# Down weights queued ahead of gate and up in the expert blocks, one down half in three passes

## The reference

```
probs = softmax(ht @ w_router)                     # 512 tokens, 16 experts
e_idx = top 2 inside the best of 4 groups
...
def expert_block(args):
    xb, e = args                                   # rows of one block, its expert
    return (silu(xb @ w1[e]) * (xb @ w3[e])) @ w2[e]
# w1, w3: 1024 x 512 (gate, up); w2: 512 x 1024 (down)
...
out = segment_sum(ys * slot_w, slot_tok)
```

## Time and profile before

| | |
|---|---|
| runs of the kernel before | 3133.07 us median of 3 (3132.41 to 3136.28) |
| the profiled execution | 3134.4 us, its span 3132.8 us |
| PE busy | 2995.8 us (96%) |
| DVE busy | 1664.4 us (53%) |
| ACT busy | 1266.9 us (40%) |
| POOL busy | 1091.5 us (35%) |
| moved | 501.22 MB, mean 160 GB/s |
| expert blocks | from about 2637 us of the span to 3093 us |

### The profile page before, as it was taken

How to read it: one execution, slowest core, us unless ns; L and a number is a source line. 1 busy time by engine, 2 the same in 40 slices (tenths; PEclk the granted TensorE clock), 3 DMA queues, 4 the chain that set the end, 5 groups by cost and what they waited for, 6 DMA issues and landing times. The chain is left out here.

```text
span 3132.8 us, 35850 instructions
## 1 busy us (share of the span) xinstructions
PE 2995.8 (96%) x13604; PEld 2278.2 (73%) x13604; DVE 1664.4 (53%) x2818; ACT 1266.9 (40%) x1920; POOL 1091.5 (35%) x538
## 2 busy tenths in 40 slices
PE   6899999999989999999999999999999998999998
PEld 4676677888866667788887677878777886666664
DVE  5577673222246758432213663656777146666664
ACT  4365434223245553422324454323444234554443
POOL 1242344444423324344342654444444431000001
PEclk9999999999999999999998999999999999999999
DMA  6122563433421137474332333733432325899995
GB/s 231 54 61 75 181 199 111 148 127 101 118 81 55 61 101 242 127 305 149 95 115 77 132 122 115 225 90 113 120 112 68 94 101 229 329 381 382 381 381 208
DMA packets 188504, 501.22 MB, mean 160 GB/s; under 512 B 20080, under 2 KB 98032, under 8 KB 172224
## 3 DMA queue, kind: packets, MB, share of 16 engines
q1 hardware_dynamic: 165808, 417.24, 39.4%
q0 software_dynamic: 13200, 49.32, 4.0%
q10 hardware_dynamic: 9344, 32.61, 3.0%
HBM read 463.83 MB, written 35.29 MB: 159 GB/s over the span
## 5 line engine op out<-in xcount | busy, mean ns | idle before, releaser
L3089 POOL TENSOR_TENSOR w_lo<-ring,w_hi 128x1024 fp32r<-128x1024 f32 (+1 forms) x375 | 900.2, 2403 | 1370.3 <-ACT w_hi L1574 1370.1
L745 PE MATMUL banks<-h_lo,w_hi 128*128 128x512 f32 x2104 | 824.8, 392 | 0.0
L1574 ACT ACTIVATE w_hi<-ring 128x1024 fp32r<-128x1024 f32 (+1 forms) x375 | 388.7, 1038 | 545.9 <-DMA ring<-in_w_all 471.0
L744 PE MATMUL banks<-hx_hi,w_hi 128*128 128x512 f32 (+2 forms) x1400 | 588.4, 420 | 12.6 <-DVE tmp L2532 6.9
L746 PE MATMUL banks<-hx_hi,w_lo 128*128 128x512 f32 (+2 forms) x1400 | 551.2, 394 | 0.0
L745 PEld LDWEIGHTS banks<-h_lo,w_hi 128*128 128x128 f32 x2104 | 397.2, 189 | 86.7 <-issue 10.2
L744 PEld LDWEIGHTS banks<-hx_hi,w_hi 128*128 128x128 f32 (+2 forms) x1400 | 264.7, 189 | 126.9 <-issue 56.5
L746 PEld LDWEIGHTS banks<-hx_hi,w_lo 128*128 128x128 f32 (+2 forms) x1400 | 264.3, 189 | 60.4 <-issue 0.2
L744 PE MATMUL banks<-hf_hi,w_hi 128*128 128x512 f32 x704 | 274.7, 390 | 0.7 <-DVE h_lo L2255 0.7
L746 PE MATMUL banks<-hf_hi,w_lo 128*128 128x512 f32 x704 | 274.0, 389 | 0.0
L2574 DVE TENSOR_TENSOR arena<-sgs,banks 128x512 f32<-128x512 f32 x44 | 30.3, 689 | 314.5 <-PE banks L746 314.5
(11 more groups left out here) (462 smaller groups left out, 5163.1 us busy)
## 6 DMA issues: line engine op xcount, KB each, us to landing
ring<-in_w_all SPq DMA_DIRECT2D x352, 512.0 KB, 3.9
arena<-in_w_all SPq DMA_DIRECT2D x26, 2048.0 KB, 14.0
arena<-in_w_all SPq DMA_DIRECT2D x100, 512.0 KB, 4.9
ring<-in_w_all SPq DMA_DIRECT2D x46, 1024.0 KB, 7.4
arena<-in_w_all SPq DMA_DIRECT2D x25, 1024.0 KB, 9.3
x<-in_w_all SPq DMA_DIRECT2D x23, 1024.0 KB, 9.5
abuf<-in_w_all SPq DMA_DIRECT2D x32, 512.0 KB, 5.0
routed<-abuf POOLq DMA_DIRECT2D x1, 12288.0 KB, 52.2
```

Of the source, the lines that this page charges most:

```text
L744: pe.matmul(bank[0:m, :], upper, hi, start=first, stop=False)
L745: pe.matmul(bank[0:m, :], upper, lo, start=False, stop=False)
L1574: act.activation(hi_at(u)[:, 0:n], raw_at(u)[:, 0:n], ACT.Copy).then_inc(w_upper, 1)
L3089: pool.tensor_tensor(lo_at(u)[:, 0:n], raw_at(u)[:, 0:n], hi_at(u)[:, 0:n], ALU.subtract)\
```

## The change

- SP: inside the loop over blocks, `down_in(b-1)` now stands ahead of `gate_and_up(b)`.
- PE: in blocks 1 to 21 the first down half (columns 0 to 511) stays a float32 product, the second (512 to 1023) is taken in three passes of halves, 12 matmuls; it waits for `hid_split`. Blocks 0 and 22 keep `down_block`.
- ACT: `upper_down(b-1)` makes the upper halves of the hidden rows (512 columns) and of the second down half (two of 1024). It stands at the start of `step(b)`, ahead of `gate_half(b)`, and waits for `hidb` and for the down load.
- DVE: `lower_down(b-1)` makes the lower halves (one of 512, two of 1024) at the start of `block_step(b)`, ahead of unit 0's, and waits for all three ACT instructions. The lower half of the weights is written over the weights; the upper halves have room of their own in `arena`.

```diff
@@ SP
             for b in range(3, N_BLK):
+                down_in(b - 1, (b - 1) % 2, b - 1)
                 if b == E_N:
                     router_told(sp, "experts_known")
                 gate_and_up(b)
-                down_in(b - 1, (b - 1) % 2, b - 1)
             down_in(N_BLK - 1, 0, N_BLK - 1)
@@ PE
+            def down_half(half, par):
+                for k in range(4):
+                    mm = pe.matmul(sc_b[half], hidb[:, k * P:(k + 1) * P],
+                                   down[par][:, k * D + half * SEQ:k * D + (half + 1) * SEQ],
+                                   start=(k == 0), stop=(k == 3))
+                return mm
+            def split_down_block(b, par):
+                pe.wait_ge(sem("wd_in%d" % par), 8 * (b - par) + 16)
+                pe.wait_ge(sem("hidden_in"), b + 1)
+                pe.wait_ge(sem("yd2_done"), b + 1)
+                down_half(0, par)
+                pe.wait_ge(sem("hid_split"), 3 * b + LAYERS * FF_T)
+                for k in range(4):
+                    rows_hi, rows_lo = hidb_hi[:, k * P:(k + 1) * P], hidb_lo[:, k * P:(k + 1) * P]
+                    pe.matmul(sc_b[1], rows_hi, down_hi[:, k, :], start=(k == 0), stop=False)
+                    pe.matmul(sc_b[1], rows_hi, down_lo[par][:, k, :], start=False, stop=False)
+                    mm = pe.matmul(sc_b[1], rows_lo, down_hi[:, k, :], start=False, stop=(k == 3))
                 mm.then_inc(sem("d_done"), 1)
@@ ACT
+            def upper_down(b, par):
+                act.wait_ge(sem("hidden_in"), b + 1)
+                act.activation(hidb_hi, hidb, ACT.Copy).then_inc(sem("hid_upper"), 1)
+                act.wait_ge(sem("wd_in%d" % par), 8 * (b - par) + 16)
+                for k in range(0, 4, 2):
+                    act.activation(down_hi[:, k:k + 2, :], down_raw[par][:, k:k + 2, :], ACT.Copy).then_inc(sem("hid_upper"), 1)
-            def step(b):
+            def step(b, par=None):
                 act.wait_ge(sem("hidden"), b)
+                if par is not None:
+                    upper_down(b - 1, par)
                 gate_half(b)
@@ DVE
+            def lower_down(b, par):
+                dve.wait_ge(sem("hid_upper"), 3 * b + LAYERS * FF_T)
+                TT(hidb_lo, hidb, hidb_hi, SUB).then_inc(sem("hid_split"), 1)
+                for k in range(0, 4, 2):
+                    TT(down_lo[par][:, k:k + 2, :], down_raw[par][:, k:k + 2, :], down_hi[:, k:k + 2, :], SUB)\
+                        .then_inc(sem("hid_split"), 1)
-            def block_step(b, par, first=False):
+            def block_step(b, par, first=False, split=True):
+                if split:
+                    lower_down(b - 1, 1 - par)
                 lower_weights(b + 1, (0,))
```

More of the change, by code:

```diff
@@ L468, in two_blocks @@
         htok = part(QT, D)
+        wdown_at = cursor[0]
         wdown = part(4 * D)
@@ L480, in two_blocks @@
         down = [wdown, flat(merged2)]
+        blocks_of = lambda v: v.rearrange("p (a b) -> p a b", b=D)[:, :, SEQ:D]
+        down_raw = [blocks_of(v) for v in down]
+        down_lo = [blocks_of(halves("down_lo%d" % n, "arena", at, 4 * D)) for n, at in enumerate((wdown_at, 0))]
+        split_at = -(-cursor[0] // 64) * 64
+        down_hi = halves("down_hi", "arena", split_at, 4, SEQ)
+        hidb_hi, hidb_lo = (halves("hidb_%s" % n, "arena", split_at + at, SEQ) for n, at in (("hi", 4 * SEQ), ("lo", 5 * SEQ)))
+        print("SPLIT", split_at, ARENA, shared_end)
         SLOT = 4 * UNIT
@@ L1486, in down_block @@
                 pe.wait_ge(sem("yd2_done"), b + 1)
[L1487 to L1491, removed]
+                down_half(0, par)
+                down_half(1, par).then_inc(sem("d_done"), 1)
+            def split_down_block(b, par):
+                pe.wait_ge(sem("wd_in%d" % par), 8 * (b - par) + 16)
+                pe.wait_ge(sem("hidden_in"), b + 1)
+                pe.wait_ge(sem("yd2_done"), b + 1)
+                down_half(0, par)
+                pe.wait_ge(sem("hid_split"), 3 * b + LAYERS * FF_T)
[4 more added lines that the diff above has]
+                    mm = pe.matmul(sc_b[1], rows_lo, down_hi[:, k, :], start=False, stop=(k == 3))
                 mm.then_inc(sem("d_done"), 1)
@@ L1506, in _ @@
                 if b == 2:
-                    down_block(1, 1)
+                    split_down_block(1, 1)
                 turn_hidden(b)
@@ L1514, in _ @@
                     rows_in(b + 1, n)
-                    down_block(b - 1, n)
+                    split_down_block(b - 1, n)
                     turn_hidden(b)
@@ L2179, in step @@
                 upper_weights(b + 1, (2, 3))
-            for b in (1, 2):
-                step(b)
+            step(1)
+            step(2, 1)
             with act.Fori(1, (N_BLK - 1) // 2 - 1) as i:
                 for n in range(2):
-                    step(2 * i + (n + 1))
-            step(N_BLK - 2)
+                    step(2 * i + (n + 1), n)
+            step(N_BLK - 2, 0)
             act.wait_ge(sem("hidden"), N_BLK - 1)
+            upper_down(N_BLK - 2, 1)
             gate_half(N_BLK - 1)
@@ L3051, in _ @@
             for b in (1, 2):
-                block_step(b, b % 2, True)
+                block_step(b, b % 2, True, b == 2)
             with dve.Fori(1, (N_BLK - 1) // 2 - 1) as i:
@@ L3056, in _ @@
             block_step(N_BLK - 2, 1)
+            lower_down(N_BLK - 2, 1)
             gated_block(N_BLK - 1)
```

## The result

The changed kernel takes **3147.1 us** (median of 7 runs, 3141.3 to 3152.1) against 3134.3 us before (7 runs, 3131.5 to 3139.3): a ratio of 1.0041, with a 95% interval from 1.0031 to 1.0051. It is slower by 0.4%, 12.8 us. I had forecast 3125.4 us, a gain, with a range up to 3136.0. The prediction is wrong in sign.

What follows compares the result with a forecast made beforehand. It took PE and the DMA engines as both full; blocks of 18.85 us instead of 19.18 over 19 periods save 6.3 us, plus 1.4 from blocks 1 and 21: -7.7 us, giving 3125.4 us, range 3118.0 to 3136.0.

Steps and rivals of the forecast that it cites:

- the second path: From unit 1's landing to the next block's lowered rows, 4.65 us; gives a 19.0 us block, or 17.5 in another.
- Part 3: Work put on DVE: 2.9 us a block plus standstill for ACT's 2.5; serial paths give 18.8 to 19.0 us a block.
- Part 4: SP's queue: down load issued ahead of unit 0, in time for ACT, but queue depth lost: a quarter microsecond idle a block.
- Part 1: Second down half on PE as 12 matmuls: saves 0.70 us a block, 14.7 us at most over 21 blocks.
- The gap: DMA idleness between unit 3 and the later down load: 0.25 us a block, ends nothing and 0.8 us.
- What the DMA engines can do: Time the transfers need for a block's 7.37 MB: between 17.3 and 19.1 us, taken as 18.6.
- full already: Rival: transfers need 19.1 us a block, so the loop stays there; 3130.2 us in all, chance 0.30.
- The long serial path: From ACT's start on unit 3 through hidden rows, ACT and DVE work to the next block's lowered rows: some 17.2 us.
- DVE as full as PE: With the new lowering work and the standstill for ACT, DVE comes to 18.3 us a block.
- The wait of PE on the lowered rows: Sign of being right: PE waits some 0.4 us a block for the lowered rows.
- The gap case: Rival: transfers need 19.1 us and also idle 0.5 before the down load; 19.6 a block, 3139.7 us, chance 0.14.
- The first rival: PE remains the bound in the block loop, so all 14.7 us are gained: 3118.4 us, chance 0.18.

Runs made afterwards that it cites:

- e1: Kernel before the change with only the new SP order (down load ahead of gate and up), no split and no new ACT or DVE work: 3141.6 us.
- e2: Changed kernel with SP's old order, the down load behind unit 3: 3134.1 us, ratio 0.9994 to the kernel before.
- e6: Changed kernel with SP's old order and the next block's rows raised and lowered ahead of unit 1: 3120.9 us, ratio 0.9948 to the kernel before.
- e7: Changed kernel with rows ahead of unit 1 and the second down half multiplied as float32, new ACT and DVE work kept: 3131.5 us.
- e9: Changed kernel with the down load issued between units 1 and 2: 3166.9 us, ratio 1.0101 to the kernel before.
- e5: Kernel before the change with only the rows raised and lowered ahead of unit 1: 3129.7 us, ratio 0.9982.
- e4: Changed kernel, new order kept, with the next block's rows raised and lowered ahead of unit 1: 3120.4 us, ratio 0.9949 to the kernel before.
- e3: Changed kernel with all new ACT and DVE work and waits, but PE multiplies the second down half as float32: 3141.3 us, ratio 1.0010.

## Why the prediction was wrong

**The step that failed: the second path.** I found the loop through unit 1 in Part 3 (unit 1 lands, the rows are lowered 4.65 us later) and closed it with "The change does not shorten this path". That was true, and the wrong question: the change lengthened it. I took unit 1's landing at S + 12.8 to 14.3 as given, though Part 4 moved 2 MB directly ahead of units 0 and 1 and Part 1 asked for the same bytes in less time. On average it lands at S + 15.4 in after, S + 13.9 in before. L went from 8.1 to 9.15 us, which by 10.6 + L raises the waiting period from 18.7 to 19.75. Five blocks at half clock, whose unit 1 is issued 1.3 to 1.7 us later, add 0.43 us to the mean, and the four that end otherwise 0.14: that makes the 20.32. It took the order and the split together: either alone leaves L at 7.9 or 8.1 (e1, e2). What in the queue makes L grow when both are there was not isolated.

**The gap (Part 4) was put in the wrong sum.** I priced the lost depth of the queue at 0.25 us of DMA idleness a block, added to what the transfers need. The idleness is real (98 GB/s at 2814, DMA share 0.94 against 0.99), but it isn't an addend: it delays exactly the unit on which the start of the next block hangs, which delays the issue of the unit after that. My upper end for it, 0.8 us a block, was under the 1.5 us by which 20.33 exceeds 18.85.

**What the DMA engines can do** was mis-sized too: I took 18.6 us a block from the distance of two landings and gave 0.30 to "full already" on a share of 0.99. e6 moves the same 7.37 MB in 18.45 us at 398 GB/s. At a share of 0.99 the engines had more to give; they went at the pace at which they were asked. By the Trainium skill, "DMA: Bandwidth & Descriptors", section Specifications, some 358 GB/s is a core's limit from HBM, a stack's 716 divided by its two cores; e6's row of a kernel on one core disagrees, as the earlier trace rows did. Its fabric ceiling of 435 GB/s is contradicted by no row of 320 us here.

**What held.** The passes (Part 1): 0.70 us a block foreseen, 19.10 to 18.45 = 0.65 measured from e7 to e6, and 11 us of the at most 14.7 in the median. The long serial path: 17.2 us foreseen, 17.2 read in e9, and it ends ten of e2's blocks, at a period near the 19.0 that I gave it. DVE as full as PE at 18.3 us: in e6 DVE copies the hidden rows at 2783.30 and again at 2801.59, 18.29 us apart, and starves nobody. PE doesn't wait for hid_split in after. The work on ACT and DVE is covered where the rows hang on unit 0 (e7 against e5). The wait of PE on the lowered rows was foreseen at 0.4 us a block and is 22.3 / 18 = 1.2, and that did not hold.

**The rivals.** The gap case had the right sign and the right place, SP's queue between unit 3 and the down load. Its price was 19.6 us a block where 20.3 came, its mechanism (the engines' capacity plus a pause) was not the one found, and its condition, that the transfers need over 18.7 us, was not met: they need at most 18.45. Its chance of 0.14 was too low, because I had tied the danger to capacity and not to latency. The first rival, PE stays the bound, is what e4 and e6 became: 3120.4 and 3120.9 us against its 3118.4. It needed one edit that the change doesn't have.

**The clock** was in no part of the sum. In after the five waits of 2.0 us and more at the start of a block went with the five drops and the shorter ones with none, so those waits were dearer than their own length. The length of one wait doesn't decide it: e3 has PE idle for 2.2 us and e9 for 2.9 (2803.2 to 2806.1), each at a clock of 1.00 and with no drop behind it.

```profile
2784.50:2786.70 2.20, 0.07 (x1) 0.00 (x0) 2.20 (x4) 1.88 (x3) 0.00 (x0) 1.00 0.86 227
```

**Two slips** in the prediction changed no step. By its own sum, 18.75 to 19.0 us a block is 3123.5 to 3128.2 us and not 3122.5 to 3127.3; and slice 35 of the page has 8 tenths and 329 GB/s, so that 381 holds from slice 36 on the earlier trace rows.

**What stays open.** The 5 to 6 us that the order alone costs (e1) show in the median and in the scatter but not in its one profile. The granted clock doesn't explain them: e1's executions of 3139.4, 3141.2 and 3141.7 us have the 0.983 of its fastest. Its profile has one block behind unit 1, 19.67 us with L at 9.12; more of these, as in e3, would do it, but no profile shows them. How the 12.4 us of added PE busy time (343.65 against 18 x 18.40 = 331.2) divide beyond the 8.2 us of half clock was not tried. The gain of e6 over e2 wasn't divided between the two paths that the edit relieves. A down load cut in two transfers with a unit between them was not tried either.

## What to carry to other kernels

Before you move a transfer in a queue, write down for each transfer behind it who waits for its landing and whether that wait closes a loop with its own issue; such a loop costs latency, and a faster engine doesn't shorten it. When a faster engine brings nothing, look for what its next stage really hangs on: here, taking the rows out from behind a 1 MB unit they had no need of was worth 0.2% alone and turned the loss of 0.4% into a gain of 0.5%. A DMA share of 0.99 says that the engines had work, not that they could do no more.

## What the runs showed of the hardware that I had not expected

- The same transfers, the same packets: 381 GB/s at a share of 0.99 before, 398 GB/s at 1.00 in e6, over 320 us or more each. The share doesn't measure how near the rate is to its limit.
- PE's clock fell to 1.2 GHz for 3.4 us some time *after* PE had resumed in four of the five drops: 1.4 us (idle until 2794.6, half clock from 2796.0), 1.3, 1.2 and 0.4; in the fifth, at 2956.4, 0.6 us before. So most of the price falls on the block that has just begun late.
- A saving on PE, the engine that bounded the kernel before, made the changed one slower: e3 with 0.7 us more PE work a block runs in 3141.3 us, after in 3147.1.
